# Thirteen more chunks of the FFN down projections in seven block products, and two of their four block sums made by adding DMAs

## The reference

```python
f = jnp.square(jax.nn.relu(h @ w_ff1[l])) @ w_ff2[l]
```

## Time and profile before

| | |
|---|---|
| median of three executions | 2538.45 us |
| profiled execution, time | 2540.52 us |
| profiled execution, span of the core's instructions | 2538.7 us |
| granted TensorE clock, mean | 0.998 |
| busy: TensorE matmul, VectorE, ScalarE, GpSimd | 99%, 74%, 48%, 0% |
| DMA | 567 MB, mean 223 GB/s |

### The profile page before, as it was taken

The page is one execution under the profiler, slowest core; times in us unless marked ns, Lnnn a source line. Parts: engine busy times, 40 slices in busy tenths (PEclk is TensorE's granted clock), DMA queues, the critical chain, the costliest instruction groups (busy, mean ns, idle before and its releaser), DMA issues.

```text
span 2538.7 us, 30593 instructions
## 1 busy us (share of the span) xinstructions
PE 2506.8 (99%) x12230; PEld 2092.1 (82%) x12230; DVE 1872.8 (74%) x2564; ACT 1227.8 (48%) x1791; POOL 6.4 (0%) x16
## 2 busy tenths in 40 slices
PE   7999999999999999999999999999999999999998
PEld 4887888888877888888888888888788888888886
DVE  7987998788887866557876865556765578778687
ACT  4544354533456444434544566455564444444454
POOL 0000000000000000000000000000000000000000
PEclk9999999999999999999999999999999999999999
DMA  9984376598985775555555645544555555555553
GB/s 399 414 334 166 118 274 259 198 343 320 348 314 216 282 297 200 190 186 191 196 199 183 212 178 183 192 140 149 185 181 198 187 195 198 190 188 205 181 201 147
DMA packets 78749, 567.14 MB, mean 223 GB/s; under 512 B 8800, under 2 KB 8928, under 8 KB 10256
## 3 DMA queue, kind: packets, MB, share of 16 engines
q1 hardware_dynamic: 77472, 558.09, 60.0%
q0 software_dynamic: 1136, 7.10, 0.7%
HBM read 563.06 MB, written 2.10 MB: 223 GB/s over the span
## 4 chain that ended last, share of the span: by engine, by line
PE 88%; DVE 6%; DMA 4%; ACT 1%; issue 1%; SPq 0%; DVEq 0%; ACTq 0%
PE ps L1309 18%; PE ps L1312 18%; PE ps L1310 18%; PE ps L1404 16%; PE ps L1415 8%; DMA raw<-stream_in 3%; DVE wl L2202 2%; DVE ACC L2314 1%; PE ps L1347 1%; PE ps L1345 1%; PE ps L1344 1%; DMA M<-stream_in 1%; ACT wh L1761 1%; DVE ACC L2301 1%; PE ps L1437 1%
## 5 line engine op out<-in xcount | busy, mean ns | idle before, releaser
L2202 DVE TENSOR_TENSOR wl<-raw,wh 128x1024 fp32r<-128x1024 f32 (+1 forms) x800 | 942.2, 1219 | 277.9 <-ACT wh L1761 275.5
L1761 ACT ACTIVATE wh<-raw 128x1024 fp32r<-128x1024 f32 (+1 forms) x800 | 801.9, 1050 | 610.4 <-PE ps L1312 464.9
L1309 PE MATMUL ps<-wh,U 128*128 128x512 f32 x1200 | 469.6, 391 | 0.0
L1312 PE MATMUL ps<-wl,U 128*128 128x512 f32 x1200 | 467.9, 390 | 0.9 <-DVE wl L2202 0.8
L1310 PE MATMUL ps<-wh,U 128*128 128x512 f32 x1200 | 467.0, 389 | 0.0
L1404 PE MATMUL ps<-HT,wh 128*128 128x512 f32 x1792 | 432.0, 392 | 0.0
L1309 PE MATMUL ps<-wh,HT 128*128 128x512 f32 x1080 | 430.4, 399 | 0.2 <-DVE HT L2375 0.2
L1312 PE MATMUL ps<-wl,HT 128*128 128x512 f32 x1080 | 422.7, 391 | 1.2 <-DVE wl L2202 1.1
L1310 PE MATMUL ps<-wh,HT 128*128 128x512 f32 x1080 | 421.5, 390 | 0.0
L1404 PEld LDWEIGHTS ps<-HT,wh 128*128 128x128 f32 x1792 | 328.5, 188 | 64.4 <-issue 1.1
L1312 PEld LDWEIGHTS ps<-wl,U 128*128 128x128 f32 x1200 | 225.2, 188 | 50.4 <-DVE wl L2202 3.4
(11 more groups left out here) (341 smaller groups left out, 1957.5 us busy)
## 6 DMA issues: line engine op xcount, KB each, us to landing
raw<-stream_in SPq DMA_DIRECT2D x524, 1024.0 KB, 4.8
M<-rows_in POOLq DMA_DIRECT2D x6, 1024.0 KB, 5.1
M<-stream_in SPq DMA_DIRECT2D x3, 1024.0 KB, 11.5
y_out<-X SPq DMA_DIRECT2D x3, 512.0 KB, 2.6
X<-x_in SPq DMA_DIRECT2D x1, 1024.0 KB, 5.2
X<-x_in SPq DMA_DIRECT2D x2, 512.0 KB, 15.3
raw<-stream_in SPq DMA_DIRECT2D x1, 640.0 KB, 5.8
raw<-stream_in SPq DMA_DIRECT2D x1, 512.0 KB, 4.0
```

What stands on the lines that cost most here:

```text
L1309: e.matmul(o, ah, H[:, c:c + bw], start=k == k0, stop=False)
L1312: ins = e.matmul(o, ah, L[:, c:c + bw], start=False, stop=end)
L1761: e.activation(H, raw[place[n][0]][:, c:c + w], ACT.Copy).then_inc(*hi.tick(p))
L2202: e.tensor_tensor(L, raw[place[n][0]][:, c:c + w], H.bitcast(F32), ALU.subtract).then_inc(*lo.tick(p))
```

## The change

- `SEVEN` has 31 chunks instead of 18: all eight down slabs of both nets now have some. New are fd00 (3, 5), fd01 (2, 5), fd10 (2, 4), fd11 (1, 3), gd00 (3, 5) and gd01 (1, 3, 5); fd21 has (2, 4) instead of (1, 3).
- Of the four weight sums, two are made by DMA from the GpSimd queue. One DMA brings block 0 of the chunk into a part of M (two buffers, in turn), a second adds block 1 to it as it arrives; a third adds block 3 to block 1 in place in the raw buffer, once the chunk has landed. VectorE makes the two other sums. The parts are cut anew: part 0 is blocks 0 and 2, part 1 is block 1 after the addition and block 3, part 2 the DMA's sum (512 columns), part 3 the two sums of VectorE. The raw buffer is free after part 2.
- The blocks k of a slab are taken in another order, so that the combined activations of a group serve both its slabs; up to three pairs are kept. The ring of float tiles shrinks from 4 to 2. The lows of the combined activations are written by three instructions into three places instead of one.
- In group 0 the results of the seven products are written to the output first, by ScalarE and VectorE, and the four banks of the ordinary products are then added by VectorE (before: two copied by ScalarE, two by VectorE).
- The 16 `w_ada` chunks of the first net stand elsewhere (`BESIDE_F`).
- The row R_GPF is loaded after the last such chunk of fd11 instead of before fu01. Scratch space of `rotary` moves from M to QKT.

The core of the diff:

```diff
-SEVEN = {"fd20": (1, 3), "fd21": (1, 3), "fd30": (1, 3), "fd31": (1,), "gd10": (1, 3), "gd11": (1, 3),
+SEVEN = {"fd00": (3, 5), "fd01": (2, 5), "fd10": (2, 4), "fd11": (1, 3), "fd20": (1, 3), "fd21": (2, 4),
+         "fd30": (1, 3), "fd31": (1,), "gd00": (3, 5), "gd01": (1, 3, 5), "gd10": (1, 4), "gd11": (1, 3),
          "gd20": (1, 3), "gd21": (1, 3), "gd30": (1, 3), "gd31": (1,)}
...
+BESIDE_F = {"fu00": "6", "fu01": "034", "fd00": "17", "fd01": "37", "fu10": "0346", "fu11": "1457"}
...
-    mixed([f"f{p}{g}{s}" for g in range(4) for p in "ud" for s in range(2)],
-          [("a", c, j) for c in (5 * D, 5 * D + 1024) for j in range(8)], 2, skip=2)
+    ada = [("a", c, j) for c in (5 * D, 5 * D + 1024) for j in range(8)]
+    for s in [f"f{p}{g}{s}" for g in range(4) for p in "ud" for s in range(2)]:
+        beside([("g", s, i) for i in range(8)], ada, [int(str(i) in BESIDE_F.get(s, "")) for i in range(8)])
...
-        if by_seven(name, i) and j == 0:
+        if by_seven(name, i) and j == 2:
             add("blocksums", n)
...
-            return lo(last_piece[n] - 2 if by_seven(*events[n][1:]) else last_piece[n])
+            return lo(last_piece[n] - 1 if by_seven(*events[n][1:]) else last_piece[n])
...
+        def sums_in(begin, end):
+            for j, n in enumerate(seven_events):
...
+                if before is not None:
+                    e.wait_ge(*lo(last_piece[before] - 1))
+                if name[2] == "0" and not buffer:
+                    e.wait_ge(*combine_f((name[0], 0, 0)))
+                if buffer:
+                    e.wait_ge(*combine_l((name[0], int(name[2]))))
+                e.dma_start(first_sum(n), p).then_inc(first_in, 16)
+                e.wait_ge(first_in, 16 * (j + 1))
+                e.dma_start(first_sum(n), q, accum_op=ALU.add).then_inc(with_second(n)[0], 16)
+                e.wait_ge(*arrived(n))
+                e.dma_start(four(n)[:, 1, :], s, accum_op=ALU.add).then_inc(in_place(n)[0], 16)
...
+        sums_in(("f", 0), ("f", 2))
+        n = last_seven(events.index(("g", "fu20", 0)))
+        if n is not None:
+            e.wait_ge(*gemm(("piece", last_piece[n])))
         e.dma_start(Mu(6, 2), rows[R_GPF].partition_broadcast(128)).then_inc(row_in[R_GPF], 16)
+        sums_in(("f", 2), ("g", 0))
...
-            products = {0: [(4, *mine(k, 0)), (0, *mine(k + 1, 0))], 1: [(1, *sums(3))],
-                        2: [(5, *sums(0)), (7, *sums(1))], 3: [(6, *sums(2)), (2, *mine(k + 1, 1))]}[pieces[p]["part"]]
+            products = {0: [(4, *mine(k, 0)), (0, *mine(q, 0))], 1: [(7, *sums(1)), (1, *sums(3))],
+                        2: [(5, *sums(0))], 3: [(6, *sums(2)), (2, *mine(q, 1))]}[pieces[p]["part"]]
...
-                if pieces[p]["part"] > 1:
-                    e.wait_ge(*blocksum((n, pieces[p]["part"])))
+                if pieces[p]["part"] == 1:
+                    e.wait_ge(*in_place(n))
+                if pieces[p]["part"] == 2:
+                    e.wait_ge(*with_second(n))
+                if pieces[p]["part"] == 3:
+                    e.wait_ge(*blocksum((n, 3)))
...
+            e.wait_ge(*in_place(n))
+            e.tensor_tensor(SUMS[:, 0:512], b[:, 512:1024], b[:, 0:512], ALU.add).then_inc(*blocksum.tick((n, 1)))
             e.wait_ge(*blocksum((n, 1)))
-            e.tensor_tensor(SUMS[:, 1536:2048], SUMS[:, 1024:1536], b[:, 1024:1536], ALU.add).then_inc(*blocksum.tick((n, 3)))
+            e.tensor_tensor(SUMS[:, 512:1024], SUMS[:, 0:512], b[:, 1024:1536], ALU.add).then_inc(*blocksum.tick((n, 3)))
...
+                for q, a in LOWS:
+                    low = a.rearrange("p (q r n) -> p q r n", q=q.stop - q.start, r=MOST)[:, :, 0:many, :]
+                    e.tensor_tensor(low, v[:, q], h[:, q].bitcast(F32), ALU.subtract).then_inc(
+                        *combine_l.tick(*([key] if q.stop == 4 else [])))
```

More of the change, by code:

```diff
@@ L1023, in seven_source @@
         part, n = pieces[p]["part"], pieces[p]["n"]
[L1024 to L1034, removed]
-    COMBINED_H, COMBINED_L = MR[:, 6144:7168], MR[:, 7168:8192]
@@ new lines, in seven_source, with first_place @@
+        return (first_sum(n) if part == 2 else SUMS), H
+    seven_events = [n for n in range(len(events)) if events[n][0] == "g" and by_seven(*events[n][1:])]
+    def first_place(n):
+        buffers = [sum(events[m][1][:3] == events[k][1][:3] for m in seven_events if m < k) % 2 for k in seven_events]
+        buffer = buffers[seven_events.index(n)]
+        used = [m for m, b in zip(seven_events, buffers) if m < n and b == buffer]
+        return M[:, 512 * buffer:512 * buffer + 512], buffer, len(used), used[-1] if used else None
@@ new lines, in first_sum, with in_place, with_second @@
+    def first_sum(n):
+        return first_place(n)[0]
+    def in_place(n):
+        i = place[n][0]
+        return third_in[i], 16 * (1 + sum(place[m][0] == i for m in seven_events if m < n))
+    def with_second(n):
+        _, buffer, uses, _ = first_place(n)
+        return second_in[buffer], 16 * (uses + 1)
+    SUMS, COMBINED, KEPT = M[:, 1024:2048], M[:, 512:512 + 512 * MOST], M[:, 2560:4096]
+    COMBINED_H = MR[:, 6144:6144 + 512 * MOST]
+    LOWS = ((slice(0, 1), MR[:, 7680:7680 + 128 * MOST]), (slice(1, 3), ACCR[:, 1024:1024 + 256 * MOST]),
+            (slice(3, 4), RTR[:, 0:128 * MOST]))
@@ L1049, in stage, with combined, last_seven @@
+    def combined(kind, r):
+        low = next((a, kind - q.start) for q, a in LOWS if q.start <= kind < q.stop)
+        c = 128 * (MOST * low[1] + r)
+        return COMBINED_H[:, 128 * (MOST * kind + r):128 * (MOST * kind + r) + 128], low[0][:, c:c + 128]
+    def last_seven(n):
+        used = [m for m in range(n) if events[m][0] == "g" and by_seven(*events[m][1:])]
+        return used[-1] if used else None
     def stage(name):
@@ L1255, in gpsimd @@
     def gpsimd(e):
+        def sums_in(begin, end):
+            for j, n in enumerate(seven_events):
+                _, name, i = events[n]
+                if not begin <= (name[0], int(name[2])) < end:
+                    continue
+                off, w = offs[n]
+                p, q, _, s = (stream[off:off + 128 * w].rearrange("(p r n) -> p r n", p=128, r=4)[:, r, :] for r in range(4))
+                _, buffer, _, before = first_place(n)
+                if before is not None:
[9 more added lines that the diff above has]
+                e.dma_start(four(n)[:, 1, :], s, accum_op=ALU.add).then_inc(in_place(n)[0], 16)
         e.dma_start(CT[:, 0:C_COS], consts[:, 0:C_COS]).then_inc(const_in, 16)
```

213 lines of the change are left out of this document (126 added, 87 removed).

## The result

The changed kernel takes 2555.95 us (median of four executions, 2554.17 to 2562.79), beside 2538.2 us for the kernel before in the same session: the ratio is 1.0072, 95% interval 1.0059 to 1.0085. It is slower by some 18 us where 8 us less were forecast. It lies outside the range, and slower had been given a chance of 0.12. Its profiled execution is the longest of the four, 2562.79 us with a span of 2561.0 us; before it was 2540.52 and 2538.7, so the two profiles stand 22.3 us apart.

The account below looks back on a forecast made before the run. TensorE, busy 99% of the span, was taken as the bound: -8.84 us for 39 matmuls fewer plus 0.6 us of stall gave -8.2 us, so 2530.2 us from the median of 2538.45, range 2528.8 to 2535.5.

Parts of the forecast that it names:

- The condition: Third DMA, each new chunk: must land 2.1 us before TensorE begins the chunk, or TensorE waits; 0.6 us forecast at fd00 3.
- I take 6 us, nearer to the low end: Landing of the adding DMA: 6 us, between bounds of 4.6 or 5.1 and 8.0 us; 0.6 us of stall.
- It starts when the load has landed: Third DMA of a chunk: the addition in place was taken to start at its load's landing, with no queue delay.
- the first two only need part 2's conversion to come after them: First two DMAs of a chunk: two landings in series, 5 us each, fit before the sum is needed; no cost.
- The allowances: Time for the third DMA to land without a stall: 10.3 us at fd20 3, 5.3 at fd00 3, 6.4 at fd01 5.
- The gain, -8.84: TensorE: 13 further chunks with 3 matmuls less each, 39 x 0.2267 = 8.84 us saved, the whole gain.
- The 18 old chunks give nothing more: Chunks already in seven products: no further gain, since they already run without a gap at 4.76 us.
- Rival 2: Adding DMAs land late everywhere: all gain lost at 10.4 us, about 2590 us at 12 us; chance 0.12.
- Rival 1: Tight places (additions landing after 8 us in the first net) and VectorE give back half: 2534.9 us; chance 0.14.
- VectorE's overrun in fu11: VectorE where combination and w_ada meet: may overrun by 1 to 2 us; TensorE loses 0 to 1 us, taken as 0.
- Rival 3: GpSimd's DMA issues wait for VectorE's current instruction, up to 1.3 us each: 2.9 us back, 2532.5 us; chance 0.08.
- Rival 4: TensorE's work isn't shortened, for instance because banks 4 to 7 or group 0's evacuations delay slabs: 2538 us; chance 0.06.

Follow-up runs that it names:

- e13: Changed kernel, but SyncE issues the load following a seven-product chunk only once that chunk's third DMA has landed: 2550.74 us, ratio 1.0051 to the kernel before.
- e4: Changed kernel, but the second and third DMA copy instead of adding, so the result is not the reference's: 2542.89 us, ratio 1.0016 to the kernel before.
- e2: Changed kernel, but group 0's first DMA waits for the last turn on TensorE instead of the combination: 2553.22 us, ratio 1.0057 to the kernel before.
- e5: Changed kernel without the first two DMAs; VectorE makes that sum, from the block as added (result not the reference's): 2548.34 us, ratio 1.0039.
- e9: Changed kernel with all three DMAs, but no w_ada chunk in fd00 and fd01: 2548.88 us, ratio 1.0038 to the kernel before.
- e7: Changed kernel, but VectorE makes the sum in place and group 0's first DMA doesn't wait for the combination: 2532.66 us, ratio 0.9977.
- e10: Changed kernel with VectorE's sum in place, group 0's first DMA earlier, and no w_ada chunk in fd00 and fd01: 2532.36 us, ratio 0.9974.
- e1: Changed kernel, but VectorE adds block 3 to block 1 in place instead of the third DMA; the first two DMAs stay: 2535.32 us, ratio 0.9985.

## Why the prediction was wrong

**The condition was right, what went into it was wrong.** The prediction has it that the third DMA must land 2.1 us before TensorE begins the chunk. Worked out for all 31 chunks of the changed kernel from its timelines, "late by" (landing + 2.1 - begin, in us) is above zero for the seven that stall and for no other:

| chunk | load landed | third DMA issued | landed | chunk begun | late by | stall |
|---|---|---|---|---|---|---|
| fd00 3 | 866.70 | 868.19 | 878.27 | 874.35 | 6.0 | 6.66 |
| fd01 2 | 913.43 | 913.71 | 920.24 | 919.52 | 2.8 | 3.10 |
| fd01 5 | 933.36 | 933.65 | 941.77 | 938.58 | 5.3 | 5.59 |
| gd00 3 | 1934.79 | 1942.06 | 1951.58 | 1947.66 | 6.0 | 6.31 |
| gd01 3 | 1986.27 | 1986.56 | 1996.88 | 1995.90 | 3.1 | 3.37 |
| gd01 5 | 1999.76 | 2000.05 | 2008.75 | 2009.80 | 1.1 | 1.34 |
| gd10 4 | 2127.43 | 2127.80 | 2136.61 | 2137.43 | 1.3 | 1.57 |

In all 25.6 us, where 27.9 were measured. The sum had 0.6 us for this term. Three of its inputs failed.

**The size of the landing, the step that failed first.** "I take 6 us, nearer to the low end" was near the median (6.7), but the seven chunks that count have 6.5 to 10.3 us, six of them above my upper bound of 8.0. My rows were of a few single DMAs of GpSimd, and I chose among them: the view of the earlier trace rows also has a second DMA of 192 KB, at 7.7 us, and one of 344 KB at 6.7. The floor is 3.5 us for an addition and 2.9 for a copy, with no load beside; the loads make 6 to 10 of it, and with the loads held back it is 4.1 (e13). Adding is a small part at the floor, 0.6 us, but 1.7 us at the median beside the loads, and 16 of the 28 us of stalls (e4). What I should have asked is what SyncE does at the moment when the third DMA starts: it issues the next 1 MB.

**"It starts when the load has landed" was false in group 0.** Rows 1936.93 to 1942.06 show the third DMA leaving 7.3 us after the load's landing. I had looked at which later rows wait behind the sums in the GpSimd queue, and not at what the third DMA itself waits behind: the two first ones of its own chunk, which have waits of their own. e2 took the wait away and gd00 3's stall with it. The statement that "the first two only need part 2's conversion to come after them" hid this: they were no cost by their own landing, but they stood ahead of the one that was.

**The allowances.** They were worked out from the median of a load, 4.8 us, and for fd00 and fd01 from rows in which no chunk around was a seven-product one. fd01 2's load, issued at 904.16 and landed at 913.43, took 9.3 us, and those of gd01 3 and gd01 5 took 8.5 and 8.8. fd01 5's took only 4.7 us but was issued 9.9 us before its chunk, where the rows before had 13.3; in e5, where fd01 2 doesn't stall, it is still 10.4. So its allowance was 3.1 us and not 6.4. That the later release of the raw buffers did this, priced at "about half a us", fits, but no run tested it. I found two tight places; the change had seven. In the first net `w_ada` took part, 11.8 us of stalls by e9.

**The clock wasn't priced, and cost little.** The lower clock followed the waits of fd00 3, fd01 5 and gd00 3. Yet fd01 5 and gd00 3 stall by 0.3 us more than they are late, just as the four chunks do whose clock stayed up; fd00 3 by 0.6. My reading is that the parts behind part 1 are split only after the landing, so TensorE would have waited for them at the full clock too, as it does in fd01 2 and gd01 3, in four waits of 0.3 to 0.7 us each. Behind the chunk, fd00 took 50.5 us where e7's took 42.3 us, 1.5 more than its stall; gd00 took 48.9 beside 42.5, hardly more than its stall.

**The gain, -8.84.** The 39 matmuls are gone, but a chunk takes 4.82 and not 4.76 us, so 31 x 0.06 = 1.9 us come back, from the 18 old chunks too: "The 18 old chunks give nothing more" was so, and they give something back. And the two last slabs, with one such chunk each (fd31, gd31), take 0.5 us more each; 0.2 of it lies in the chunk itself, for the rest I have no row. -8.84 + 1.9 + 1.0 = -5.9 us is what the idea is worth without a stall. e7 and e10, without any, measured 5.8 and 6.6 us less than before by their ratios.

**The sum redone**, between the two profiled spans: -5.9 + 27.9 = +22.0, measured +22.3. The agreement is partly luck: by the starts of the slabs some 2.6 us more were lost in fd00, fd01, gd00 and gd01 right behind the stalled chunks (which of the slow clock and the late splits did it isn't shown), and 2.3 us fewer were spent in the stage before fu00, which was longer in the profile of before (slab wo1 50.38 us, 48.0 in the changed kernel). By the medians the change costs 17.8 us, since the profiled execution was the slowest of four.

**The rivals.** Rival 2 (slower, additions late everywhere) had the right sign and, in an addition that lands late, the right mechanism, but not its places: no landing reached its point of no gain, 10.4 us. The longest was 10.3, and the 24 other chunks, with landings up to 7.5 us, lost nothing or 0.2 us. What was lost came of late issues, late loads and landings of 6.5 to 10.3 us at seven chunks, not of one long landing everywhere. Rival 1 named the first net and w_ada, rightly for 15 of 28 us, at 2534.9. VectorE's overrun in fu11, taken as 0, was 0 here (the slab has 44.53 us in both) and 0.8 us in e1, which has one VectorE instruction more a chunk; e7, with as many, shows none of it. Rival 3 isn't borne out: e4's 31 issues all took 536 to 538 ns with VectorE 76% busy, so nothing held these; the 0.85 to 1.24 us of the additions go with adding. Rival 4 is refuted by e7.

**Left open.** No run told whether the loads hold the addition up in the DMA engines' queues or at SBUF, or by what the `w_ada` chunks cost where they stand. Nor is it known why the additions of e13, all without a load beside them, took 3.5 to 3.9 us in the first net and 4.1 to 4.3 in the second (the first of each net, 5.5 and 5.4). And it is open what the landings vary by between executions: e13's profiled execution took 2548.7 us, its median is 2550.7.

## What to carry to other kernels

Before work is moved to a DMA, ask whether its landing lies between a load and a waiting engine. The first two DMAs of each chunk lay beside the path and cost little by their own landings; the third lay on it and cost 20 us, and one VectorE instruction of 0.68 us did its work off the path. Price such a landing by the longest of its kind, by what the other queues issue at that moment (here the next 1 MB load), and by what stands ahead of it in its own in-order queue, waits included.

## What the runs showed of the hardware

- A DMA of 256 KB from GpSimd's queue that adds into SBUF took 0.86 us to issue (1.24 close behind another) and landed after 3.5 to 3.6 us with no load beside it, 6.3 to 8.7 with over 6 us of 1 MB loads beside it (e5), 10.3 at most with others of its queue; a copy took 0.54 us to issue and 2.9 to 3.3 with no load beside.
- The loads pay too. Their median is 4.8 us in both kernels, but the longest later than 730 us took 7.6 before the change and 10.2 with it, and fd01 2's took 9.3.
- After 3.7 us without a matmul the granted clock was 0.52 for 6.5 us, and 1.00 in the stretch after. The stalls of the three chunks with a lowered clock were at most 0.4 us longer, measured against how late their DMA landed, than those of the four without.
- Matmuls with the high part of the stationary tile in one tensor and the low part in another were spaced 0.233 us instead of 0.2267.
